# A gated delta rule on one Trainium2 core: where the state is decayed, when the query products are made, and which engine takes the convolution's centre tap

## The reference, cut to what matters

```python
qkv = silu(short_conv(concat([dq, dk, dv]), conv_w))     # 5 taps along the tokens, 3072 channels
...
def step(state, xs):                                     # 8 chunks of 64 tokens, 8 heads, both directions
    q_c, k_c, u_c, w_c, g_c, a_c = xs
    g_last = g_c[..., -1]
    v_new = u_c - einsum('bhcd,bhdv->bhcv', w_c, state)
    o = (einsum('bhcd,bhdv->bhcv', q_c * exp(g_c)[..., None], state)
         + einsum('bhcj,bhjv->bhcv', a_c, v_new))
    k_dec = k_c * exp(g_last[..., None] - g_c)[..., None]
    state = state * exp(g_last)[..., None, None] + einsum('bhcd,bhcv->bhdv', k_dec, v_new)
    return state, o
```

## Time and profile before

| | |
|---|---|
| median of 3 runs | 1859.4 us (1850.43 to 1859.76) |
| the profiled execution, its own time | 1855.62 us |
| its span (first to last instruction) | 1853.8 us |
| PE busy | 1584.7 us, 85% |
| DVE busy | 702.4 us, 38% |
| ACT busy | 381.1 us, 21% |
| POOL busy | 140.3 us, 8% |
| convolution, first to last DVE work | about 429 to 651 us |
| delta rule, `phase(2)` to `phase(3)` | about 655 to 836 us |

### The profile page before, as it was taken

How to read it: one execution, slowest core, us unless ns; L and a number is a source line. 1 busy time by engine, 2 the same in 40 slices (tenths; PEclk the granted TensorE clock), 3 DMA queues, 4 the chain that set the end, 5 groups by cost and what they waited for, 6 DMA issues and landing times. The chain is left out here.

```text
span 1853.8 us, 20991 instructions
## 1 busy us (share of the span) xinstructions
PE 1584.7 (85%) x8078; PEld 958.2 (52%) x8078; DVE 702.4 (38%) x1197; ACT 381.1 (21%) x767; POOL 140.3 (8%) x179
## 2 busy tenths in 40 slices
PE   6987888999998877879899999999989976877770
PEld 5854343444543466664344878774668763322230
DVE  2036334003479844443200043400365555222225
ACT  2112335003231245340100122301221010100101
POOL 0000000000008043320000000000000001000001
PEclk9997999999999979889999999999977978999995
DMA  5154101122221222216121221322210058999983
GB/s 187 49 159 141 59 28 46 46 68 92 68 69 46 69 69 84 78 48 238 46 91 45 69 91 46 60 68 71 91 27 24 1 207 330 425 427 425 425 364 147
DMA packets 118088, 237.44 MB, mean 128 GB/s; under 512 B 10645, under 2 KB 100339, under 8 KB 109043
## 3 DMA queue, kind: packets, MB, share of 16 engines
q1 hardware_dynamic: 111811, 212.14, 32.1%
q0 software_dynamic: 3744, 13.63, 1.9%
q10 hardware_dynamic: 2448, 10.49, 1.4%
HBM read 221.56 MB, written 14.69 MB: 127 GB/s over the span
## 5 line engine op out<-in xcount | busy, mean ns | idle before, releaser
L787 PE MATMUL pss<-arena 128*128 128x256 f32 (+1 forms) x704 | 235.0, 492 | 22.6 <-ACT arena L1412 12.6
L1412 ACT ACTIVATE arena<-pss 128x512 f32<-128x512 f32 (+1 forms) x205 | 108.4, 529 | 630.3 <-PE pss L787 553.3
L787 PE MATMUL psv<-arena,wslot 128*128 128x512 f32 x512 | 229.1, 602 | 2.8 <-DVE arena L1883 1.5
L787 PEld LDWEIGHTS pss<-arena 128*128 128x128 f32 x704 | 135.3, 195 | 114.6 <-issue 88.5
L787 PE MATMUL pss<-arena,wslot 128*128 128x512 f32 x384 | 170.1, 600 | 4.0 <-POOLq L1732 2.5
L787 PEld LDWEIGHTS psv<-arena,wslot 128*128 128x128 f32 x512 | 96.1, 191 | 119.8 <-issue 115.4
L787 PE MATMUL pss<-wslot,arena 128*128 128x256 f32 (+1 forms) x640 | 147.5, 391 | 3.5 <-issue 1.9
L1371 PE MATMUL pss<-arena 128*64 128x512 f32 x384 | 124.0, 650 | 21.6 <-DMA arena<-w_expert_in 17.7
L787 PEld LDWEIGHTS pss<-wslot,arena 128*128 128x128 f32 x640 | 120.7, 190 | 29.0 <-issue 11.7
L787 PEld LDWEIGHTS pss<-arena,wslot 128*128 128x128 f32 x384 | 73.2, 193 | 96.4 <-issue 93.6
L1883 DVE TENSOR_TENSOR arena<-arena 128x512 f32<-128x512 f32 (+5 forms) x96 | 72.2, 752 | 122.4 <-ACT arena L1412 102.9
(11 more groups left out here) (304 smaller groups left out, 1768.8 us busy)
## 6 DMA issues: line engine op xcount, KB each, us to landing
arena<-w_expert_in SPq DMA_DIRECT2D x24, 2048.0 KB, 21.7
wslot<-w_in SPq DMA_DIRECT2D x32, 1024.0 KB, 5.4
arena<-w_expert_out SPq DMA_DIRECT2D x32, 1024.0 KB, 22.7
wslot<-w_ada SPq DMA_DIRECT2D x18, 1024.0 KB, 5.2
wslot<-w_expert_in SPq DMA_DIRECT2D x8, 2048.0 KB, 21.5
arena<-w_in SPq DMA_DIRECT2D x10, 1024.0 KB, 9.0
y_dram<-arena ACTq DMA_DIRECT2D x16, 512.0 KB, 9.7
arena<-w_ada SPq DMA_DIRECT2D x6, 1024.0 KB, 7.9
```

The lines of the kernel that those rows point to most:

```text
L787: m = mm(o, l, r, start=(n == 0), stop=(n == len(pairs) - 1))
L1412: L.did(A(dst, src, func, **kw), s[sig] if sig else None, [s["free_s"]])
```

## The change

Three edits.

- **State.** The sixteen multiplications of the state on ACT are gone, and with them `sd_ready`. DVE's four additions of 128x512 become sixteen multiply-adds of 128x128 that take the decay as their scalar. A new helper `go` raises the chain semaphore without the wait after it: in these groups, in the eight value corrections and in ACT's evictions of query products, only the fourth instruction of four is waited for. `key_values` fills the banks of both directions side by side, so that both are full at the end of a half.
- **Query products.** PE makes them after `new_values` instead of before `grow`, always into `pss`. ACT evicts them after the new values and the exponential, with the scale, into the output tile (g = 0) or into `dQS`, a free piece of the arena (g = 1), and DVE adds `dQS` with one addition per half in the place of its eight multiply-adds. For n > 4 ACT waits for the previous step's output before it writes `dQS`.
- **Centre tap.** ACT makes it, as a scaled copy out of the same `psv` bank, and DVE waits for it (`tap_ready`) in front of its four multiply-adds. Sums of squares, turns and their evictions move one tile later (`i = j - 2`), and the loops have one more turn.

```diff
+    def go(self, ins):
+        ins.then_inc(self.chain, 1)
+        self.raised[self.chain] = self.raised.get(self.chain, 0) + 1
...
+        dQS = T32[:, 0, :, :].rearrange("p u c -> p (u c)").rearrange("p (h n) -> p h n", h=NH)
...
+        def conv_job(j):
+            return V_CONV + j + (j >= 2) + (j > 12) + (j > 18)
...
+                o = [bank("v"), bank("v")]
+                for h in heads(hg):
+                    m = [mm(o[x][:, (h % 4) * HD:(h % 4 + 1) * HD], dKD[HX[x], h, :], dVN[HX[x], h, :], start=True,
+                            stop=True) for x in range(2)]
                 for x in range(2):
-                    o = bank("v")
-                    for h in heads(hg):
-                        m = mm(o[:, (h % 4) * HD:(h % 4 + 1) * HD], dKD[HX[x], h, :], dVN[HX[x], h, :], start=True,
-                               stop=True)
-                    m.then_inc(s["full_v"], 1)
+                    m[x].then_inc(s["full_v"], 1)
...
-            for j in range(24 + 1):
...
-                if 1 <= j < 17:
+                i = j - 2
+                if 0 <= i < 16:
                     L.need(s["sq_ready"])
...
-                            m = mm(o[HX[x], q:q + 1], csq[:, (j - 1) % 2, chunk(q, x)], ones[:, 0:1], start=True, stop=True)
+                            m = mm(o[HX[x], q:q + 1], csq[:, i % 2, chunk(q, x)], ones[:, 0:1], start=True, stop=True)
                     m.then_inc(s["full_s"], 1)
-                if 1 <= j < 9 or j > 16:
-                    pe.wait_ge(s["silu_ready"], j)
-                    turn_chunks(kT[:, j - 1, :] if j < 9 else cst[:, (j - 1) % 2, :])
+                if 0 <= i < 8 or i >= 16:
+                    pe.wait_ge(s["silu_ready"], i + 1)
+                    turn_chunks(kT[:, i, :] if i < 8 else cst[:, i % 2, :])
...
                 if j in KK_AT:
+                    pe.wait_ge(s["silu_ready"], NH)
...
-                    for hg in range(2):
-                        with_state("v" if step_of(n)[0] else "s", qT, n, hg)
                 if more:
                     grow(n + 1)
                 for hg in range(2):
                     new_values(n, hg)
+                if n:
+                    for hg in range(2):
+                        with_state("s", qT, n, hg)
...
-            for j in range(24 + 1):
+            for j in range(24 + 2):
+                if j < 24:
+                    act.wait_ge(s["full_v"], conv_job(j) + 1)
+                    L.did(A(conv[:, j % 2, :], psv[:, conv_job(j) % 4, :], ACT.Copy, scale=tap(j, 2)), s["tap_ready"])
...
+                i = j - 2
+                if 0 <= i < 16:
+                    evict(dn_sum[:, i, :], NT, "sum_ready")
+                if 0 <= i < 8:
+                    evict(ktok[:, :, i, :], SEQ, None)
+                if i >= 16:
+                    evict(vtok[:, :, i - 16, :], SEQ, None)
...
-                if n and g == 0:
-                    for hg in range(2):
-                        b = full()
-                        for h in range(hg * 4, hg * 4 + 4):
-                            L.did(A(oacc[:, q, h, :], b[:, (h % 4) * HD:(h % 4 + 1) * HD], ACT.Copy,
-                                    scale=coef(co_eG, g, q, h)), s["qs_ready"] if h % 4 == 3 else None,
-                                  [s["free_s"]] if h % 4 == 3 else [])
                 for hg in range(2):
                     if 0 < n:
...
@@ -1582,15 +1600,18 @@
                     evict(dVN[:, hg * 4:hg * 4 + 4, :], SEQ, "vn_ready")
                 if more:
                     decays(n + 1)
-                if n and more:
+                if n:
                     for hg in range(2):
-                        act.wait_ge(s["qs_ready"], 2 * (n - 1) + hg + 1)
-                        for x in range(2):
-                            for h in range(hg * 4, hg * 4 + 4):
-                                v = state[:, x ^ g, h, :]
-                                L.did(A(v, v, ACT.Copy, scale=coef(co[:, 6 + x, :], g, q, h)),
-                                      s["sd_ready"] if h % 4 == 3 else None)
+                        if n > NCK // 2:
+                            act.wait_ge(s["o_ready"], 2 * (n - 1) + hg + 1)
+                        b = full()
+                        for h in range(hg * 4, hg * 4 + 4):
+                            o = dQS[:, h, :] if g else oacc[:, q, h, :]
+                            ins = A(o, b[:, (h % 4) * HD:(h % 4 + 1) * HD], ACT.Copy, scale=coef(co_eG, g, q, h))
+                            if h % 4 < 3:
+                                L.go(ins)
+                            else:
+                                L.did(ins, s["qs_ready"], [s["free_s"]])
...
                 b = full()
-                if j >= 2:
-                    dve.wait_ge(s["silu_ready"], j - 1)
+                L.need(s["tap_ready"])
                 o = conv[:, j % 2, :]
-                col = (j + 8) % 16 if j < 16 else j
-                taps = [ccols[:, k * 24 + col:k * 24 + col + 1] for k in range(CONV_K)]
-                scale(o, b, taps[2])
                 for k in (0, 1, 3, 4):
                     m = k - 2
                     lo, hi = max(0, -m), SEQ - max(0, m)
-                    L.did(V.scalar_tensor_tensor(o[:, lo:hi], b[:, lo + m:hi + m], taps[k], o[:, lo:hi],
+                    L.did(V.scalar_tensor_tensor(o[:, lo:hi], b[:, lo + m:hi + m], tap(j, k), o[:, lo:hi],
                                                  ALU.mult, ALU.add),
                           s["conv_ready"] if k == 4 else None, [s["free_v"]] if k == 4 else [])
...
-                            L.did(V.scalar_tensor_tensor(dVB[:, h, :], b[:, (h % 4) * HD:(h % 4 + 1) * HD],
-                                                         coef(co_ce, g, q, h), dVB[:, h, :], ALU.mult, ALU.add),
-                                  s["r_ready"] if h % 4 == 3 else None, [s["free_v"]] if h % 4 == 3 else [])
-                if g:
-                    for hg in range(2):
-                        b = full()
-                        for h in range(hg * 4, hg * 4 + 4):
-                            o, v = oacc[:, q, h, :], b[:, (h % 4) * HD:(h % 4 + 1) * HD]
-                            L.did(V.scalar_tensor_tensor(o, v, coef(co_eG, g, q, h), o, ALU.mult, ALU.add),
-                                  None, [s["free_v"], s["qs_ready"]] if h % 4 == 3 else [])
+                            ins = V.scalar_tensor_tensor(dVB[:, h, :], b[:, (h % 4) * HD:(h % 4 + 1) * HD],
+                                                         coef(co_ce, g, q, h), dVB[:, h, :], ALU.mult, ALU.add)
+                            if h % 4 < 3:
+                                L.go(ins)
+                            else:
+                                L.did(ins, s["r_ready"], [s["free_v"]])
...
                         for x in range(2):
-                            v = state[:, x ^ g, hg * 4:hg * 4 + 4, :]
-                            if n:
-                                dve.wait_ge(s["sd_ready"], 4 * (n - 1) + 2 * hg + x + 1)
+                            d = x ^ g
                             b = full()
                             if n == 0:
-                                L.did(V.tensor_copy(v, by4(b)), s["st_ready"], [s["free_v"]])
-                            else:
-                                add(v, v, by4(b), s["st_ready"], [s["free_v"]])
+                                L.did(V.tensor_copy(state[:, d, hg * 4:hg * 4 + 4, :], by4(b)), s["st_ready"],
+                                      [s["free_v"]])
+                                continue
+                            for h in range(hg * 4, hg * 4 + 4):
+                                v = state[:, d, h, :]
+                                ins = V.scalar_tensor_tensor(v, v, coef(co[:, 6 + x, :], g, q, h),
+                                                             b[:, (h % 4) * HD:(h % 4 + 1) * HD], ALU.mult, ALU.add)
+                                if h % 4 < 3:
+                                    L.go(ins)
+                                else:
+                                    L.did(ins, s["st_ready"], [s["free_v"]])
...
                     o = oacc[:, q, hg * 4:hg * 4 + 4, :]
                     if n:
                         dve.wait_ge(s["qs_ready"], 2 * (n - 1) + hg + 1)
+                    if g:
+                        add(o, o, dQS[:, hg * 4:hg * 4 + 4, :])
```

14 lines of the change are left out of this document (7 added, 7 removed).

## The result

| | before | after |
|---|---|---|
| median of four runs, us | 1854.9 (1850.1 to 1859.8) | 1806.5 (1805.9 to 1812.1) |
| profiled execution: time / span, us | 1855.6 / 1853.8 | 1812.1 / 1810.3 |
| ratio of the medians, 95% interval | | 0.9746 (0.9706 to 0.9785) |

A forecast was written before the change was run, and what follows sets the result against it. Bound: a chain of waits on ACT's state multiplications in the delta rule, DVE late in the convolution. 1855.6 - 10 (convolution) - 30.9 (loop) = 1814.7, from the median 1818.5; given as 1817 us, range 1806 to 1836.

The forecast's parts named there:

- DVE's 36.3 us: Delta rule before the change: DVE's additions waited 36.3 us in 24 pieces for ACT's decay of the state.
- The centre tap: Convolution: thirteen taps, tiles 11 to 23, leave a full DVE; value 10 us, bounds 4 and 12.
- Rival (c): Convolution gives nothing because DVE waits for taps; 1827 us, chance 0.09.
- The group of four: State update on DVE: four multiply-adds without inner waits take 1.13 us, 1.51 by the upper bound.
- rival (a): Removed waits give nothing, each DVE step in the loop stays at 0.387 us; 1823 us, chance 0.20.
- L842's wait: Loop, PE's weight load behind ACT's eviction: idle time of 5.08 us shrinks to about 0.6 us.
- Rival (b): Loop: the wait comes back in another place, such as behind query evictions, with lower clock; 1834 us, chance 0.16.
- PE idle before the query products under 1 us: Loop: a sign listed as showing the forecast right, PE's idle time ahead of these products under 1 us.
- I take the middle, 19.8, since some waits stay: Loop, a step with PE as bound: 18.6 to 21.1 us, taken as 19.8; 22.6 for n=2.
- The steps n = 6 and 7: End of the loop: DVE's chain is the bound, 27.2 us, bounds 26.0 to 30.3, against 29.7 before.
- Rival (d): Whole kernel: nothing arrives, a later transfer absorbs the gain; 1857 us, within 0.5% of before, chance 0.05.
- Rival (e): Loop: slower, TensorE stays at its half clock, seven steps cost 60 us; about 1905 us, chance 0.04.

The follow-up runs named there:

- act_filler: Changed kernel plus sixteen unread 128x128 copies on ACT in steps 1 to 6, where the state's decay stood: loop 160.3 us, 1841.9 us in one run.
- state_only: Changed kernel with waits after every instruction, key_values one direction after the other and query products in the old place: loop 124.3 us, median 1809.0.
- no_shift: Changed kernel with the convolution's squares and turns one tile behind, not two, centre tap still on ACT: convolution 219.4 us, median 1808.0.
- kv_in_turn: Changed kernel with key_values filling one direction's bank after the other, as before: loop 121.0 us, median 1803.7.
- last_q: Changed kernel with the query products back in their old place in step n=7 alone: loop 113.6 us, median 1799.0.
- q_first: Changed kernel with query products ahead of grow and their evictions ahead of the new values in every step: loop 110.9 us, median 1795.5.
- delta_only: Kernel before with only the state and query product edits, convolution as before: loop 118.5 us, median 1808.6.
- waits_back: Changed kernel with the wait after every instruction of a group of four restored: loop 132.2 us, median 1810.4.

## Why the prediction was right, and where it was off

**The bound.** Right in the main: ACT's sixteen multiplications were the price of the loop, by the wait of L842 that the earlier trace rows shows. act_filler puts ACT's work back and the loop is 160.3 us again; state_only has of the edits to the loop that one alone, with the queries' new way through ACT, and has 36.0 of the 42.3 us. The other wait that the prediction named beside it, DVE's 36.3 us, cost nothing in n = 1 to 5: act_filler does not have it.

**The centre tap.** 10 us stated, 9.1 measured. The size was right, its reasoning only in half: 13 x 0.78 was put down to DVE as the full engine, and the later tile was named as what lets PE follow. no_shift shows that without this second edit 5.5 of the 9.1 us are gone. That 10 was so near 9.1 is in part luck. Rival (c), nothing from the convolution, fell.

**The group of four.** 1.13 us came from a step of 0.26 us between two instructions, the middle of 0.133 and 0.387. Half of the fixed 0.218, as the text has it, would have been 0.24 or 0.28. No row decided for the middle, so that L2104 takes 1.13 to the hundredth is luck; the measured step, (1.13 - 0.345)/3 = 0.26, also lies above the estimate of 0.21 beside it; the sixteen updates took 2 x 1.12 + 2.39 + two gaps of 0.16, 4.9 us (5.2 stated). So rival (a), no gain from the removed waits, fell. What the prediction set against it was too weak: by its own 0.218 of 0.351 us, more than half of an instruction is no streaming, not a quarter to a half. The rival rested on a sentence of the Trainium skill, page "VectorE: DVE Perf Modes", section "The DRAIN you can't avoid", that operations chained without semaphores gain nothing, measured there on eight copies; here the trace disagrees, 1.51 against 1.13 us for the same four. The same page, in "Two Vector instructions with no wait between them", to which that section points, holds an instruction back only where operands in the same memory start in different quadrants of partitions, its own against those before it or those of the instruction in front. That can't be inside a group of instructions that all start at partition 0; by that section they overlap, and the trace agrees. I had not weighed the one section against the other.

**L842's wait.** "Shrinks to about 0.6 us": PE's idle time is 0.50 a step (with the weight load's own wait 4.9 us over five steps). Rival (b), the wait coming back in another place at 1834 us, fell, but a part of it came: PE's wait before `new_values` rose from 2.2 to 6.9 us, at n = 2 and 7, because the query products no longer fill it, and in n=7 the granted clock fell from 1.00 to 0.79. The sign "PE idle before the query products under 1 us" did not come there: 4.02 us stand before `new_values` and the products behind them.

**The steps n = 1 to 5: the term that was mis-sized.** Stated 102.2 us, measured 88.5, and this is more than the whole miss. The term that was mis-sized is "I take the middle, 19.8, since some waits stay". The parts of step 1 are head 8.7, L811 and the bubble 1.6, tail 6.7, together 17.0. Against the lower bound of 18.6:
- the head is 1.1 shorter. Of that 0.76 is `key_values` side by side, which stood in the diff and was priced in no sentence; kv_in_turn measures it to the hundredth in three steps.
- the tail is 0.5 shorter than what I scaled from rows at the lower clock (L859 takes 0.61 us, where L842 took 1.02, and L958 1.15, where L941 took 1.98).
- the middle added another 1.2 that no wait came to fill. With PE as the bound and the clock at 1.00, steps 1, 3 and 5 agree within 0.01 us.

So nearly 3 us a step were too many. For n=2 about 2.8 us over the other steps were stated, and it is 3.4 (20.4 - 17.0).

**The steps n = 6 and 7.** Stated 27.2, measured 29.5, almost the 29.7 of before. The mechanism was named, "the later query products are on the path and eat what the state gives", and last_q and q_first show it: 25.3 and 25.1 us with them early. Three things in these steps had no price. Behind PE's wait of 4.02 us the clock is lower, so that L1001 takes 1.7 and L988 0.9 us more; and DVE's addition of two SBUF operands takes 1.81 us instead of 0.69 beside POOL's operation. If each counts in full, 29.5 - 1.7 - 0.9 - 1.1 = 25.8, about the lower bound stated, 26.0. kv_in_turn and delta_only bear out the 0.9: their L988 took 1.97 us in n=7, and the step 14.7 instead of 15.9. What was not drawn from the right sentence is its conclusion: that this edit as a whole costs time. For n < 6 I priced its move at nothing, which held except at n=2; at n=6 it even helped by 0.8 us.

**The sum.** Convolution -0.9, steps 1 to 5 +13.7, steps 6 and 7 -2.3 make 10.5 us more gain than stated between the convolution's start and the loop's end. The profiled execution hid 8.2 of it in its slower start. That the median stayed within the range is luck: the loop's 42.3 us are more than the 39 that the working allowed at most, and the same kernel gave a median of 1801.4 in another lot, under the range. The stated 1817 was also 2.3 us over the sum, 1814.7, to meet a median of before of 1859.4 from three runs; with a fourth it is 1854.9. Rival (d) fell, a gain passed on whole: everything behind took 1017.9 us against 1018.1. Rival (e) fell: in after the clock rose to 1.00 in n = 1 to 6. The clock does belong to the account, though, with the other sign: in act_filler's first step it is a third of ACT's price. Its sum was also low by its own figures, 7 x 9.6 us are 67 and not 60, which decides nothing.

What stays open: why the granted clock ahead of the convolution differs from one execution to the next, how much of waits_back's 14.2 us is the waits' own and how much the clock behind them, and what the convolution's later tile is worth without the tap's move.

## What to carry to other kernels

Work off the critical path on an engine's in-order queue costs nearly its full length (here 6.0 us of idle time for 6.9 of work) where one small step that the bound engine needs stands behind it; look first at what such a step stands behind, and count the slower clock after the idle time as part of the price (here 3 us on 6). Once the wait is gone, price a step as the plain sum of the bound engine's work, every edit of the diff in it, and not as a middle between that sum and a guess at remaining waits. Work that filled another engine's wait should stay there: moving it behind cost 7 to 8.5 us in all, in two steps of seven, though in a third it filled another wait.

## What the runs showed of the hardware that was not expected

- Groups of four independent instructions overlap once the waits between them are gone, on both engines: four multiply-adds of 128x128 on DVE 1.51 to 1.13 us, four scaled copies of 128x128 on ACT from 1.62 (half of 3.25) to 1.14. One alone takes 0.345 and 0.37 us, so four in a row without overlap would be 1.38 and 1.47.
- Two products on different row halves, issued in turn matmul by matmul: 32 matmuls in 2.06 us instead of 2.82.
- A DVE addition of 128x512 with both inputs in SBUF took 1.81 us where it started 0.01 us behind a POOL operation of 1.27 us (776.95 and 776.96 above), and 0.69 us otherwise. Steps n = 4 and 5 show the same pair (1.82 and 1.81 us), off the path there. Additions with one input in PSUM kept 0.69 beside POOL. The Trainium skill, page "SBUF — State Buffer", section "SBUF: two separate sides", says that of two such operations, the one on POOL reading SBUF, the second is blocked in full until the first has ended. The trace agrees in the main: POOL ends 1.26 us after the addition's start, and 0.55 are left, somewhat less than the 0.69 of an addition alone.
- ACT's copy of 128x512 out of PSUM takes 0.69 us with its scale read from memory, and 0.60 us in the plain eviction (L1433).
